# Latent attention's steps two at a time: shared rotary scores, three rotating bank pairs, four probability buffers

## The chip, the core and the metric

The kernel runs on one core of one Trainium2 chip. Time is the device time of one execution in microseconds. TensorE multiplies matrices into PSUM, which has eight banks of 512 float32 per partition; VectorE and ScalarE work element by element; GpSimd is hardly used here; SyncE issues the transfers. Each engine runs its own queue in order, and engines wait for each other by semaphores.

## What is computed

Four layers on x of 512 tokens by 1024 channels, in float32: a sparse-attention mixer and a latent-attention mixer, each followed by a gated feed-forward layer, then a gated delta rule and a gated linear attention, each with layer norm. The change lies in the attention of the second mixer: 8 heads, causal, with a key of 128 channels plus 64 rotary channels and a value of 128.

```python
def mla_mixer(h, k, v, w_q_a, q_a_norm, w_q_b, q_norm, w_out, cos, sin):
    ...
    q = jnp.concatenate([q[..., :QK_NOPE], apply_rope(q[..., QK_NOPE:], cos, sin)], axis=-1)
    scale = (QK_NOPE + QK_ROPE) ** -0.5
    ...
    def block(s0):
        t = s0 + jnp.arange(Q_BLOCK)
        qb = lax.dynamic_slice_in_dim(q, s0, Q_BLOCK, axis=1)
        s = jnp.einsum('bqhd,bkhd->bhqk', qb, k).astype(jnp.float32) * scale
        p = masked_softmax(s, kpos[None, :] <= t[:, None])
        o = jnp.einsum('bhqk,bkhd->bqhd', p.astype(v.dtype), v)
        return o.reshape(B, Q_BLOCK, MLA_HEADS * MLA_V)
    ...
    return o @ w_out
```

## The kernel before

The order of all work is written out by hand, one function per layer and engine: `pe_mla`, `act_mla`, `dve_mla`. A wait names a semaphore and a count. The attention runs in `M_STEPS` = 16 steps. A step v is a pair of heads (`ab` 0 and 1) and a tile t of 128 query tokens; it has n = (t + 1) x 128 keys. `m_step(v)` (L1981) gives for the four head pairs t = 0, 1, 2, 3, then 3, 2, 1, 0, then both again. So the steps have 128, 256, 384, 512, 512, 384, 256, 128 keys, twice over.

A step passes through nine pieces of work:

- TensorE `scores(v)` (L2106): per head one product over the 128 plain channels (L2119, "nope"), then one over the 64 rotary channels in pieces of up to 256 keys (L2124). The rotary rows of the two heads lie in partitions 0 to 63 and 64 to 127, and their matmuls start within 7 ns of each other. A float32 product is two instructions in the trace and one in the program's order. Signals `m_scores`.
- VectorE `biased(v)` (L2503): adds the mask, copies the scores from PSUM to the buffer `mprob[v % 3]` and takes the least value per row (L2509); then a small product (L2512) that signals `m_biased`.
- ScalarE `exps(v)` (L2295): two exponentials with their sums (L2300).
- VectorE `weighted(v)` (L2514): reciprocal of the sum (L2517) and scaling (L2519). Signals `m_weighted`.
- TensorE `turn(v)` (L2127): 2 (t + 1) transposes of 128 x 128 (L2137).
- ScalarE `turned(v)` (L2304): copies them from PSUM to `mpT[v % 2]` (L2309). Signals `m_pT`.
- TensorE `values(v)` (L2140): the product with the values (L2151), 4 (t + 1) instructions in the trace, into bank 6 or 7. It waits for `m_pT` and for `m_o_split` v - 1, which is `lower_o(v - 2)`. Signals `m_valued`.
- ScalarE `upper_o(v)` (L2311, instruction L2314) and VectorE `lower_o(v)` (L2522, instruction L221, `late_parts<-ps`): the result split in a high and a low part. `lower_o` signals `m_o_split`.

Beside these, `upper_out(v)` on ScalarE (L2316, instruction L2321) and `lower_out(v)` on VectorE (L2528, instruction L221, `panel_parts`) split a sixteenth of the weights of the output projection per step. `lower_out(v)` waits for `upper_out(v)`. The output projection (`out`, L2167) follows on TensorE right behind `values(15)`.

Scores lie in bank pair 0-1 or 2-3 in turn, transposes in 4-5. The order on TensorE is scores(v + 2), turn(v), values(v - 1); on ScalarE exps(v + 1), turned(v), upper_o(v - 1), upper_out(v); on VectorE weighted(v), biased(v + 2), lower_o(v - 2), lower_out(v - 1).

Of the kernel before, what the change touches and what calls it, by code (L numbers as in the profile page):

```python
# [104 lines left out]
def build_in(nc, io, ctx):  # L105
# [1815 lines left out]
    mmin, mbias, msum = [[take(2) for _ in range(3)] for _ in range(3)]  # L1921
# [3 lines left out]
    mprob = [hT[:, 2 * b:2 * b + 2, :] for b in range(3)]  # L1925
# [78 lines left out]
    def pe_mla(pe):  # L2004
# [101 lines left out]
        def scores(v):  # L2106
            pair, t, n = m_step(v)
            if v == 0:
                pe.wait_ge(S("m_dve_saved"), TT + 1)
                pe.wait_ge(S("m_q_out"), TT + 1)  # L2110
            elif v == 1:
                pe.wait_ge(S("m_dve_saved"), TT + 2)
                pe.wait_ge(S("m_q_out"), TT + 2)
            else:
                pe.wait_ge(S("m_biased"), v - 1)
            if v == 2 * TT:
                pe.wait_ge(S("m_dve_saved"), 2 * TT)
            for ab in range(2):
                mm(ps[:, 2 * (v % 2) + ab, 0:n], qTn[:, 2 * pair + ab, tokens(t)], kTn[:, 2 * pair + ab, 0:n], start=True, stop=False, skip_group_check=True)  # L2119
            for c in range(0, n, SPAN):  # L2120
                keys = slice(c, min(c + SPAN, n))
                for ab in range(2):
                    r = slice(ab * ROPE, (ab + 1) * ROPE)
                    last = mm(ps[:, 2 * (v % 2) + ab, keys], qTr[r, pair, tokens(t)], kTr[r, pair, keys], start=False, stop=True, skip_group_check=True)  # L2124
            last.then_inc(S("m_scores"), 1)

        def turn(v):  # L2127
            pair, t, n = m_step(v)
            pe.wait_ge(S("m_weighted"), v + 1)
            if v == 0:  # L2130
                pe.wait_ge(S("m_dve_saved"), TT + 3)
                pe.wait_ge(S("m_q_out"), TT + 3)
            else:
                pe.wait_ge(S("m_pT"), v)
            for ab in range(2):
                for kt in range(t + 1):
                    last = nc.tensor.transpose(ps[:, 4 + ab, tokens(kt)], mprob[v % 3][:, ab, tokens(kt)], ident[:])  # L2137
            last.then_inc(S("m_prob_turned"), 1)
# [52 lines left out]
    def act_mla(act):  # L2191
# [103 lines left out]
        def exps(v):  # L2295
            pair, t, n = m_step(v)
            act.wait_ge(S("m_biased"), v + 1)
            for ab in range(2):
                h = 2 * pair + ab
                last = nc.scalar.activation(mprob[v % 3][:, ab, 0:n], mprob[v % 3][:, ab, 0:n], ACT.Exp, bias=mbias[v % 3][:, ab:ab + 1],  # L2300
                                            scale=q_ninv[:, t, h:h + 1], accum_out=msum[v % 3][:, ab:ab + 1])
            last.then_inc(S("m_exp"), 1)

        def turned(v):  # L2304
# [4 lines left out]
            nc.scalar.copy(mpT[v % 2][:, :, 0:n], ps[:, 4:6, 0:n]).then_inc(S("m_pT"), 1)  # L2309
# [44 lines left out]
    def dve_mla(dve, link, lower):  # L2354
# [148 lines left out]
        def biased(v):  # L2503
            pair, t, n = m_step(v)
            wait_apart(dve, "m_scores", v + 1)
            if v >= 3:
                wait_apart(dve, "m_prob_turned", v - 2)
            for ab in range(2):
                last = nc.vector.tensor_tensor_reduce(out=mprob[v % 3][:, ab, 0:n], in0=ps[:, 2 * (v % 2) + ab, 0:n], in1=causal[:, T - n:T], scale=1.0, scalar=3e38,  # L2509
# [2010 lines left out]
```

## Time and profile before

| | us |
|---|---|
| median of 3 runs (2049.18 to 2051.91) | 2049.36 |
| the profiled execution, its own time | 2050.57 |
| its span, first to last instruction | 2048.8 |
| TensorE matmuls busy, of the span | 2016.0 (98%) |
| VectorE busy | 1412.9 (69%) |
| ScalarE busy | 969.6 (47%) |
| mean granted clock of TensorE | 0.996 |
| attention steps: first score matmul starts | 788.10 |
| attention steps: first output matmul starts | 848.25 |

Matmuls overlap in the pipeline: each shows its whole passage, so that an engine that is shown busy may still start its matmuls farther apart than they need. The distance from one start to the next tells what a matmul costs, and the idle time what a wait costs beyond that. A granted clock of 1.00 is 2.4 GHz, one of 0.50 is 1.2 GHz.

### The profile page before, as it was taken

How to read it: one execution, taken by the hardware profiler on the slowest of the kernel's cores; microseconds unless marked ns; L12 is line 12 of the kernel's file. 1: busy time of each engine (PE TensorE's matmuls, PEld its weight loads, DVE VectorE, ACT ScalarE, POOL GpSimd, SP SyncE). 2: the span in 40 equal slices, each digit the busy share in tenths (PEclk: the TensorE clock that was granted, in tenths of full speed). 3: DMA queues.
4: the chain of work that ended last, by engine and by line, in shares of the span. 5: the costliest groups of instructions: out<-in, count | busy, mean ns of one | idle time of the engine just before them, and what ended most of it. 6: DMA issues, size and time to landing. Idle time of an engine off the chain costs nothing. (4 is left out here: it accounts for less than half of the span.)

```text
span 2048.8 us, 36832 instructions
## 1 busy us (share of the span) xinstructions
PE 2016.0 (98%) x14803; PEld 1757.7 (86%) x14803; DVE 1412.9 (69%) x2747; ACT 969.6 (47%) x1874; POOL 148.3 (7%) x136
## 2 busy tenths in 40 slices
PE   9999999999999999999999999999999999999997
PEld 8997877999988877789999887888888888788986
DVE  5248865988865677578887556776667666586566
ACT  5337973555400266545553004554434454466554
POOL 1113320000000400000000002000000000020000
PEclk9999999999999999999999999999999999999999
DMA  5240001333232221022333321211112110212211
GB/s 189 83 145 22 2 2 65 111 104 103 94 124 96 97 70 60 22 82 93 104 107 113 109 94 67 88 63 62 61 61 72 53 59 20 91 53 102 81 44 42
DMA packets 30664, 159.35 MB, mean 78 GB/s; under 512 B 3392, under 2 KB 3904, under 8 KB 17856
## 3 DMA queue, kind: packets, MB, share of 16 engines
q1 hardware_dynamic: 30240, 157.24, 21.7%
q8 instruction: 97, 1.59, 0.3%
q14 instruction: 39, 0.32, 0.1%
q10 hardware_dynamic: 288, 0.20, 0.0%
HBM read 155.33 MB, written 2.10 MB: 77 GB/s over the span
## 5 line engine op out<-in xcount | busy, mean ns | idle before, releaser
L231 PE MATMUL ps<-late_parts,panel_upper 128*128 128x256 f32 (+1 forms) x1376 | 458.6, 333 | 0.0
L230 PE MATMUL ps<-late_parts,panel_upper 128*128 128x256 f32 (+1 forms) x1260 | 430.5, 342 | 3.8 <-issue 1.8
L232 PE MATMUL ps<-late_parts,panel_parts 128*128 128x256 f32 (+1 forms) x1260 | 424.3, 337 | 0.0
L221 DVE TENSOR_TENSOR panel_parts<-panel_sb,panel_upper 128x512 fp32r<-128x512 f32 (+1 forms) x330 | 321.1, 999 | 13.9 <-ACT panel_upper L768 8.4
L230 PE MATMUL ps<-panel_upper,hT_parts 128*128 128x256 f32 (+2 forms) x964 | 295.3, 306 | 2.2 <-DVE h_lower L961 1.4
L232 PE MATMUL ps<-panel_upper,h_lower 128*128 128x256 f32 (+2 forms) x964 | 283.7, 294 | 0.0
L231 PE MATMUL ps<-panel_parts,hT_parts 128*128 128x256 f32 (+2 forms) x964 | 282.3, 293 | 0.0
L231 PEld LDWEIGHTS ps<-late_parts,panel_upper 128*128 128x128 f32 x1376 | 258.7, 188 | 25.8
L230 PEld LDWEIGHTS ps<-late_parts,panel_upper 128*128 128x128 f32 x1260 | 236.7, 188 | 34.6 <-issue 4.5
L232 PEld LDWEIGHTS ps<-late_parts,panel_parts 128*128 128x128 f32 x1260 | 237.8, 189 | 28.6
L230 PE MATMUL ps<-hT_parts,panel_upper 128*128 128x512 f32 (+1 forms) x492 | 191.8, 390 | 1.7 <-PEq L4326 1.7
L230 PEld LDWEIGHTS ps<-panel_upper,hT_parts 128*128 128x128 f32 x964 | 183.0, 190 | 6.9 <-issue 3.2
L232 PE MATMUL ps<-hT_parts,panel_parts 128*128 128x512 f32 (+1 forms) x492 | 186.1, 378 | 0.0
L232 PEld LDWEIGHTS ps<-panel_upper,h_lower 128*128 128x128 f32 x964 | 183.2, 190 | 3.0
L231 PEld LDWEIGHTS ps<-panel_parts,hT_parts 128*128 128x128 f32 x964 | 182.2, 189 | 3.5
L231 PE MATMUL ps<-h_lower,panel_upper 128*128 128x512 f32 x416 | 165.8, 399 | 0.0
L1626 ACT CAST panel_upper<-panel_sb 128x512 fp32r<-128x512 f32 x230 | 132.3, 622 | 19.2 <-DVE panel_sb L1747 11.0
L230 PEld LDWEIGHTS ps<-hT_parts,panel_upper 128*128 128x128 f32 x492 | 92.3, 188 | 25.0 <-issue 3.9
L232 PEld LDWEIGHTS ps<-hT_parts,panel_parts 128*128 128x128 f32 x492 | 92.4, 188 | 19.5
L231 PEld LDWEIGHTS ps<-h_lower,panel_upper 128*128 128x128 f32 x416 | 78.2, 188 | 17.3 <-issue 0.2
L901 ACT ACTIVATE arena_sb<-arena_sb 128x384 f32<-128x384 f32 (+3 forms) x128 | 70.5, 553 | 9.0 <-DVE arena_sb L1160 8.7
L3206 DVE SCALAR_TENSOR_TENSOR arena_sb<-ps,arena_sb 128x511 f32<-128x511 f32 (+2 forms) x96 | 71.9, 748 | 3.4
(544 smaller groups left out, 3693.9 us busy)
## 6 DMA issues: line engine op xcount, KB each, us to landing
panel_sb<-ffn_gate_up_w SPq DMA_DIRECT2D x76, 512.0 KB, 4.5
panel_sb<-gdn_w SPq DMA_DIRECT2D x24, 1024.0 KB, 4.8
panel_sb<-ffn_down_w SPq DMA_DIRECT2D x22, 1024.0 KB, 4.8
panel_sb<-nsa_w SPq DMA_DIRECT2D x13, 1024.0 KB, 4.8
panel_sb<-gla_w SPq DMA_DIRECT2D x12, 1024.0 KB, 4.9
panel_sb<-gdn_out_w SPq DMA_DIRECT2D x8, 1024.0 KB, 4.9
panel_sb<-ffn_gate_up_w SPq DMA_DIRECT2D x6, 1024.0 KB, 4.9
panel_sb<-nsa_out_w SPq DMA_DIRECT2D x4, 1024.0 KB, 4.8
```

Source lines behind the costliest of these rows:

```text
L221: return engine.tensor_tensor(out, src, hi.bitcast(F32), ALU.subtract)
L230: mm(out, w_hi, x_hi, start=start, stop=False, skip_group_check=skip_group_check)
L231: mm(out, w_hi, x_lo, start=False, stop=False, skip_group_check=skip_group_check)
L232: return mm(out, w_lo, x_hi, start=False, stop=stop, skip_group_check=skip_group_check)
L901: nc.scalar.activation(prob[v % NB][:, ab, at:at + n], prob[v % NB][:, ab, at:at + n], ACT.Exp, bias=pmin[v % NB][:, k:k + 1], scale=-1.0, ...
L1626: nc.scalar.copy(hi, plain).then_inc(S("ffn_high"), 1)
L3206: last = nc.vector.scalar_tensor_tensor(conv[n][:, back:T], src[:, 0:T - back], hconv[:, n, 3 - back:4 - back], conv[n][:, back:T], ALU.mu ...
```

## The change

Two steps form a block. TensorE issues both nope products, then both steps' rotary products, then both groups of transposes, then two groups of values. Each use of a bank pair, scores or transposes, takes the next of three pairs (banks 0 to 5) in the order in which TensorE comes to them; `await_pair` waits for the release of the use three before: `m_biased` where that was scores, `m_pT` where it was transposes. There are four buffers `mprob` and four sets of the small sums. ScalarE and VectorE issue their pieces in twos as well. No instruction is added or removed.

The core of the diff (the changes that only put `MB` for 3 in an index are left out, except in `biased`):

```diff
+    MB = 4
+    mmin, mbias, msum = [[take(2) for _ in range(MB)] for _ in range(3)]
...
+    M_TURN, M_SCORE = "turn", "score"
+    M_SHARED = [(M_SCORE, 0), (M_SCORE, 1)]
+    for two in range(0, M_STEPS, 2):
+        M_SHARED += [(M_SCORE, v) for v in (two + 2, two + 3) if v < M_STEPS] + [(M_TURN, two), (M_TURN, two + 1)]
+    M_BANKS = {use: 2 * (n % 3) for n, use in enumerate(M_SHARED)}
+
+    def await_pair(pe, use):
+
+        n = M_SHARED.index(use)
+        if n < 3:
+            pe.wait_ge(S("m_dve_saved"), TT + 1 + n)
+            pe.wait_ge(S("m_q_out"), TT + 1 + n)
+            return
+        kind, v = M_SHARED[n - 3]
+        if kind == M_SCORE:
+            pe.wait_ge(S("m_biased"), v + 1)
+        else:
+            pe.wait_ge(S("m_pT"), v + 1)
...
+        def scores(*steps):
+            for v in steps:
+                pair, t, n = m_step(v)
+                await_pair(pe, (M_SCORE, v))
+                if v == 2 * TT:
+                    pe.wait_ge(S("m_dve_saved"), 2 * TT)
                 for ab in range(2):
...
+                    mm(ps[:, M_BANKS[M_SCORE, v] + ab, 0:n], qTn[:, 2 * pair + ab, tokens(t)], kTn[:, 2 * pair + ab, 0:n], start=True, stop=False, skip_group_check=True)
+            for v in steps:
+                pair, t, n = m_step(v)
+                for c in range(0, n, SPAN):
+                    keys = slice(c, min(c + SPAN, n))
+                    for ab in range(2):
+                        r = slice(ab * ROPE, (ab + 1) * ROPE)
+                        last = mm(ps[:, M_BANKS[M_SCORE, v] + ab, keys], qTr[r, pair, tokens(t)], kTr[r, pair, keys], start=False, stop=True, skip_group_check=True)
+                last.then_inc(S("m_scores"), 1)
...
-        for v in range(M_STEPS):
+        for v in range(0, M_STEPS, 2):
             if v + 2 < M_STEPS:
-                scores(v + 2)
+                scores(v + 2, v + 3)
             turn(v)
-            if v >= 1:
+            turn(v + 1)
+            if v:
                 values(v - 1)
+            values(v)
         values(M_STEPS - 1)
...
         exps(0)
-        for v in range(M_STEPS):
-            if v + 1 < M_STEPS:
-                exps(v + 1)
-            turned(v)
-            if v >= 1:
+        exps(1)
+        for v in range(0, M_STEPS, 2):
+            for u in (v, v + 1):
+                if u + 2 < M_STEPS:
+                    exps(u + 2)
+                turned(u)
+            if v:
                 upper_o(v - 1)
+            upper_o(v)
             upper_out(v)
+            upper_out(v + 1)
         upper_o(M_STEPS - 1)
...
-            if v >= 3:
-                wait_apart(dve, "m_prob_turned", v - 2)
+            if v >= MB:
+                wait_apart(dve, "m_prob_turned", v - MB + 1)
...
-        for v in range(M_STEPS):
+        for v in range(0, M_STEPS, 2):
             weighted(v)
+            weighted(v + 1)
+            if v >= 4:
+                lower_o(v - 3)
+            if v >= 2:
+                lower_o(v - 2)
             if v + 2 < M_STEPS:
                 biased(v + 2)
-            if v >= 2:
-                lower_o(v - 2)
+                biased(v + 3)
             if v:
+                lower_out(v - 2)
                 lower_out(v - 1)
+        lower_out(M_STEPS - 2)
         lower_out(M_STEPS - 1)
-        lower_o(M_STEPS - 2)
-        lower_o(M_STEPS - 1)
+        for v in range(M_STEPS - 3, M_STEPS):
+            lower_o(v)
```

Line numbers shift: nope L2119 is L2133 in the changed kernel, rotary L2124 is L2140, transposes L2137 are L2149, values L2151 are L2163, ScalarE's exponentials L2300 are L2314, its copies L2309, L2314 and L2321 are L2323, L2328 and L2335, VectorE's L2509, L2517 and L2519 are L2527, L2535 and L2537.

TensorE, steps 4 and 5, before: scores(4), turn(2), values(1), scores(5), turn(3), values(2).

```order
L2119 MATMUL ps<-late_sb 128x512 x2
L2124 MATMUL ps<-arena_sb 128x256 x4
L2137 MATMUL ps<-ident_sb,hT_sb 128x128 x6
L2151 MATMUL ps<-arena_sb 128x128 x4
L2119 MATMUL ps<-late_sb 128x384 x2
L2124 MATMUL ps<-arena_sb 128x256 x2
L2124 MATMUL ps<-arena_sb 128x128 x2
L2137 MATMUL ps<-ident_sb,hT_sb 128x128 x8
L2151 MATMUL ps<-arena_sb 128x128 x6
```

Now, the block for v = 2, with scores(5) drawn ahead of turn(2).

```order
L2133 MATMUL ps<-late_sb 128x512 x2
L2133 MATMUL ps<-late_sb 128x384 x2
L2140 MATMUL ps<-arena_sb 128x256 x6
L2140 MATMUL ps<-arena_sb 128x128 x2
L2149 MATMUL ps<-ident_sb,hT_sb 128x128 x14
L2163 MATMUL ps<-arena_sb 128x128 x10
```

The rotary products of steps 4 and 5 stand together behind both nope products, then come both groups of transposes and both groups of values.

ScalarE, before, around the same steps: exps(3), turned(2), upper_o(1), upper_out(2), exps(4), turned(3), upper_o(2), upper_out(3).

```order
L2300 ACTIVATE hT_sb,arena_sb<-hT_sb,arena_sb 128x512 x2
L2309 COPY arena_sb<-ps 128x2x384
L2314 CAST late_parts<-ps 128x2x128
L2321 CAST panel_upper<-panel_sb 128x512
L2300 ACTIVATE hT_sb,arena_sb<-hT_sb,arena_sb 128x512 x2
L2309 COPY arena_sb<-ps 128x1024
L2314 CAST late_parts<-ps 128x2x128
L2321 CAST panel_upper<-panel_sb 128x512
```

Now, the block for v = 2: exps(4), turned(2), exps(5), turned(3), upper_o(1) and (2), upper_out(2) and (3).

```order
L2314 ACTIVATE hT_sb,arena_sb<-hT_sb,arena_sb 128x512 x2
L2323 COPY arena_sb<-ps 128x2x384
L2314 ACTIVATE hT_sb,arena_sb<-hT_sb,arena_sb 128x384 x2
L2323 COPY arena_sb<-ps 128x1024
L2328 CAST late_parts<-ps 128x2x128 x2
L2335 CAST panel_upper<-panel_sb 128x512 x2
```

turned(2), the copy of 2x384, has exps(3) ahead of it before and exps(4) now, and the splitting of two steps comes behind both copies.

VectorE, the end of the stretch, before: lower_out(12), weighted(14), lower_o(12), lower_out(13), weighted(15), lower_o(13), lower_out(14) and (15), lower_o(14) and (15).

```order
L221 TENSOR_TENSOR panel_parts<-panel_sb,panel_upper 128x512
L2517 RECIPROCAL arena_sb<-arena_sb 128x2
L2519 TENSOR_SCALAR hT_sb<-hT_sb,arena_sb 128x256 x2
L221 TENSOR_TENSOR late_parts<-ps,late_parts 128x2x128
L221 TENSOR_TENSOR panel_parts<-panel_sb,panel_upper 128x512
L2517 RECIPROCAL arena_sb<-arena_sb 128x2
L2519 TENSOR_SCALAR hT_sb<-hT_sb,arena_sb 128x128 x2
L221 TENSOR_TENSOR late_parts<-ps,late_parts 128x2x128
L221 TENSOR_TENSOR panel_parts<-panel_sb,panel_upper 128x512 x2
L221 TENSOR_TENSOR late_parts<-ps,late_parts 128x2x128 x2
```

Now: lower_out(10) and (11), weighted(14), weighted(15), lower_o(11) and (12), lower_out(12) to (15), lower_o(13) to (15).

```order
L221 TENSOR_TENSOR panel_parts<-panel_sb,panel_upper 128x512 x2
L2535 RECIPROCAL arena_sb<-arena_sb 128x2
L2537 TENSOR_SCALAR hT_sb<-hT_sb,arena_sb 128x256 x2
L2535 RECIPROCAL arena_sb<-arena_sb 128x2
L2537 TENSOR_SCALAR hT_sb<-hT_sb,arena_sb 128x128 x2
L221 TENSOR_TENSOR late_parts<-ps,late_parts 128x2x128 x2
L221 TENSOR_TENSOR panel_parts<-panel_sb,panel_upper 128x512 x4
L221 TENSOR_TENSOR late_parts<-ps,late_parts 128x2x128 x3
```

lower_o(13) has moved behind lower_out(14) and lower_out(15).

## Rows read from the trace of the kernel before

**Rows 1.** Busy time: stretch, us, busy us (count) per engine, PEclk, DMA share, GB/s
```profile
806.00:842.00 36.00, 36.00 (x257) 27.93 (x256) 27.36 (x101) 28.12 (x68) 0.00 (x0) 1.00 0.01 1
1813.50:1816.90 3.40, 3.40 (x18) 3.40 (x17) 3.37 (x4) 2.85 (x4) 3.24 (x3) 0.50 0.00 0
```

**Rows 2.** Waits, 786 to 850 us: who waits for whom, total us, times, longest
```profile
DVE hT_sb L2509 <- PE ps L2124: 10.8, 13, 1.6
```

**Rows 3.** TensorE in time: start, us, line, count; L2119 nope, L2124 rotary, L2137 transposes, L2151 values
```profile
838.64 1.95 PE L2151 MATMUL ps<-arena_sb 128*128 128x128 f32 x16
840.43 0.61 PE L2119 MATMUL ps<-late_sb 128*128 128x128 f32 x4
840.97 0.49 PE L2124 MATMUL ps<-arena_sb 64*128 64x128 f32 x4
841.39 0.87 PE L2137 MATMUL ps<-ident_sb,hT_sb 128*128 128x128 f32 x6
842.10 1.95 PE L2151 MATMUL ps<-arena_sb 128*128 128x128 f32 x16
844.19 0.66 PE L2137 MATMUL ps<-ident_sb,hT_sb 128*128 128x128 f32 x4
844.68 1.50 PE L2151 MATMUL ps<-arena_sb 128*128 128x128 f32 x12
846.71 0.44 PE L2137 MATMUL ps<-ident_sb,hT_sb 128*128 128x128 f32 x2 [0.53 <-DVE hT_sb L2519]
846.99 1.50 PE L2151 MATMUL ps<-arena_sb 128*128 128x128 f32 x12
```

**Rows 4.** TensorE in time, three other places
```profile
793.90 0.44 PE L2137 MATMUL ps<-ident_sb,hT_sb 128*128 128x128 f32 x2 [0.24 <-DVE hT_sb L2519]
...
818.53 0.70 PE L2124 MATMUL ps<-arena_sb 64*128 64x256 f32 x4
...
825.10 1.14 PE L2124 MATMUL ps<-arena_sb 64*128 64x256 f32 x8
```

**Rows 5.** Groups by shape, 788 to 848.5 us: busy us, mean ns of one, idle before
```profile
L2300 ACT ACTIVATE hT_sb<-hT_sb,arena_sb 128x512 f32<-128x512 f32 x8 | 6.5, 812 | 0.0
...
L2300 ACT ACTIVATE hT_sb<-hT_sb,arena_sb 128x384 f32<-128x384 f32 x8 | 5.6, 702 | 0.0
L2509 DVE CUSTOM_DVE_ANT_0 hT_sb<-ps,arena_sb 128x512 f32<-128x512 f32 x8 | 5.2, 689 | 3.7 <-PE ps L2124 3.7
L2300 ACT ACTIVATE hT_sb<-hT_sb,arena_sb 128x256 f32<-128x256 f32 x8 | 4.7, 592 | 0.0
...
L2509 DVE CUSTOM_DVE_ANT_0 hT_sb<-ps,arena_sb 128x384 f32<-128x384 f32 x8 | 4.1, 555 | 1.6 <-PE ps L2124 1.6
...
L2309 ACT COPY arena_sb<-ps 128x768 f32<-128x768 f32 x4 | 3.2, 791 | 2.1 <-PE ps L2137 2.1
L2509 DVE CUSTOM_DVE_ANT_0 hT_sb<-ps,arena_sb 128x256 f32<-128x256 f32 x8 | 3.2, 423 | 2.7 <-PE ps L2124 2.6
...
L2509 DVE CUSTOM_DVE_ANT_0 hT_sb<-ps,arena_sb 128x128 f32<-128x128 f32 x8 | 2.0, 289 | 2.9 <-PE ps L2124 2.9
...
L2309 ACT COPY arena_sb<-ps 128x256 f32<-128x256 f32 x4 | 1.5, 372 | 1.3 <-PE ps L2137 1.3
```

**Rows 6.** VectorE in time: one biased of 512 keys, and the stretch's end
```profile
826.54 0.69 DVE L2509 CUSTOM_DVE_ANT_0 hT_sb<-ps,arena_sb 128x512 f32<-128x512 f32 x1 [0.70 <-PE ps L2124]
...
827.89 0.16 DVE L2512 TENSOR_TENSOR arena_sb<-arena_sb 128x2 f32<-128x2 f32 x1
...
849.01 0.69 DVE L221 TENSOR_TENSOR panel_parts<-panel_sb,panel_upper 128x512 fp32r<-128x512 f32 x1 [1.08 <-ACT panel_upper L2321]
849.62 0.75 DVE L221 TENSOR_TENSOR late_parts<-ps,late_parts 128x256 fp32r<-128x256 f32 x2
```

**Rows 7.** ScalarE in time: upper_o and upper_out at the stretch's end
```profile
848.08 0.37 ACT L2314 CAST late_parts<-ps 128x256 fp32r<-128x256 f32 x1 [0.52 <-PE ps L2151]
848.35 0.63 ACT L2321 CAST panel_upper<-panel_sb 128x512 fp32r<-128x512 f32 x1
```

More of the change, by code:

```diff
@@ L1924, in build_in @@
     rope_b = h_raw[:, 6, :]
-    mprob = [hT[:, 2 * b:2 * b + 2, :] for b in range(3)]
+    mprob = [hT[:, 2 * b:2 * b + 2, :] for b in range(MB)]
     mpT = [h_raw[:, 2 * b:2 * b + 2, :] for b in range(2)]
@@ L2129, in turn @@
             pe.wait_ge(S("m_weighted"), v + 1)
[L2130 to L2134, printed above, removed]
+            await_pair(pe, (M_TURN, v))
             for ab in range(2):
                 for kt in range(t + 1):
-                    last = nc.tensor.transpose(ps[:, 4 + ab, tokens(kt)], mprob[v % 3][:, ab, tokens(kt)], ident[:])
+                    last = nc.tensor.transpose(ps[:, M_BANKS[M_TURN, v] + ab, tokens(kt)], mprob[v % MB][:, ab, tokens(kt)], ident[:])
             last.then_inc(S("m_prob_turned"), 1)
@@ L2308, in turned @@
                 act.wait_ge(S("m_valued"), v - 1)
-            nc.scalar.copy(mpT[v % 2][:, :, 0:n], ps[:, 4:6, 0:n]).then_inc(S("m_pT"), 1)
+            nc.scalar.copy(mpT[v % 2][:, :, 0:n], ps[:, M_BANKS[M_TURN, v]:M_BANKS[M_TURN, v] + 2, 0:n]).then_inc(S("m_pT"), 1)
         def upper_o(v):
@@ L2505, in biased @@
             wait_apart(dve, "m_scores", v + 1)
-            if v >= 3:
-                wait_apart(dve, "m_prob_turned", v - 2)
+            if v >= MB:
+                wait_apart(dve, "m_prob_turned", v - MB + 1)
             for ab in range(2):
-                last = nc.vector.tensor_tensor_reduce(out=mprob[v % 3][:, ab, 0:n], in0=ps[:, 2 * (v % 2) + ab, 0:n], in1=causal[:, T - n:T], scale=1.0, scalar=3e38,
-                                                      op0=ALU.add, op1=ALU.min, accum_out=mmin[v % 3][:, ab:ab + 1])
+                last = nc.vector.tensor_tensor_reduce(out=mprob[v % MB][:, ab, 0:n], in0=ps[:, M_BANKS[M_SCORE, v] + ab, 0:n], in1=causal[:, T - n:T], scale=1.0, scalar=3e38,
+                                                      op0=ALU.add, op1=ALU.min, accum_out=mmin[v % MB][:, ab:ab + 1])
             link(last)
-            nc.vector.tensor_tensor(mbias[v % 3], mmin[v % 3], q_inv[:, t, 2 * pair:2 * pair + 2], ALU.mult).then_inc(S("m_biased"), 1)
+            nc.vector.tensor_tensor(mbias[v % MB], mmin[v % MB], q_inv[:, t, 2 * pair:2 * pair + 2], ALU.mult).then_inc(S("m_biased"), 1)
         def weighted(v):
@@ L2516, in weighted @@
             dve.wait_ge(S("m_exp"), v + 1)
-            link(nc.vector.reciprocal(msum[v % 3], msum[v % 3]))
+            link(nc.vector.reciprocal(msum[v % MB], msum[v % MB]))
             for ab in range(2):
-                last = nc.vector.tensor_scalar(mprob[v % 3][:, ab, 0:n], mprob[v % 3][:, ab, 0:n], msum[v % 3][:, ab:ab + 1], None, ALU.mult)
+                last = nc.vector.tensor_scalar(mprob[v % MB][:, ab, 0:n], mprob[v % MB][:, ab, 0:n], msum[v % MB][:, ab:ab + 1], None, ALU.mult)
             last.then_inc(S("m_weighted"), 1)
```

24 lines of the change are left out of this document (2 added, 22 removed).

## The prediction, made before the changed kernel had run

> **What bounds the kernel now.** I read the stretch in which the changed lines run, from the first score matmul (788.1 us) to the first output matmul (848.2 us), in four views: busy time by stretch, the waits, TensorE's instructions in time, and the groups of each tile shape. In the middle 36 us TensorE is busy for all 36 at the full clock, VectorE for 27 and ScalarE for 28 [rows 1]. VectorE is the one that waits, 13 times, for the last rotary matmul of a step [rows 2]. So TensorE bounds the stretch: what is taken off its queue shortens the kernel, and what makes it wait lengthens it. After the stretch its matmuls follow on without a gap, so I carry a shift here to the end whole.
>
> Busy is not the same as streaming. Four score matmuls of 128 columns take 840.43 to 840.97, 0.54 us, where 16 value matmuls of 128 columns take 838.64 to 840.43, 0.112 each, so four should take 0.45 [rows 3]. The 0.09 is the step from 128-row matmuls to 64-row ones. The rotary group of four 256-column matmuls takes 0.70 and that of eight 1.14 [rows 4]: two more pairs cost 0.44, 0.22 a pair. So a pair streams at 0.11 per 128 columns. But two pairs of 128 hold the engine from 840.97 to 841.39, 0.42 instead of 0.22 [rows 3]: 0.20 more, which goes, as the group of eight shows no more of it than that of four, to the start of the group and the way back. The first transpose costs 0.05 more than the next: two take 0.28 (846.71 to 846.99), and six against four 0.71 against 0.49, so 0.11 each [rows 3]. One excursion into rotary matmuls and back costs 0.09 + 0.20 + 0.05, with roundings 0.35 us.
>
> **What the change removes.** Before there are 16 excursions, one per step. Steps 0 and 1 keep theirs, the other 14 share seven: 7 x 0.35 = **-2.46 us**. If half of the 0.20 is paid again at the second step, it is -1.8. The trace shows it once in a group of two pairs and once in one of four [rows 3, 4], so I take the whole.
>
> The Trainium skill, "TensorEngine Tiling (Array Packing)", Key Properties, says that a change of tiling mode drains TensorE. By that rule alone a switch would cost the last matmul's depth, which I estimate from the matmul groups as 0.275 - 0.112 = 0.16, two per excursion, and the removal would be 2.3 instead of 2.46; the trace agrees in kind, and its number is used.
>
> TensorE's own idle time before is small: 0.24 and a late load, together 0.30, ahead of the first transposes (793.90) [rows 4], 2.09 - 1.79 = 0.30 ahead of those of step 14, and 2.03 - 12 x 0.112 = 0.69 ahead of those of step 15 [rows 3]. In the new order more matmuls lie ahead of all three. **-1.29 us**.
>
> **What it adds: a chain inside each block.** The block for steps v, v+1 is on TensorE: scores(v+2, v+3), turn(v), turn(v+1), values(v-1), values(v). Two of its parts now need something that starts only when rotary scores of this very block are done. turn(v+1) takes the bank pair of scores(v+2), so it waits for biased(v+2). values(v) waits for the copy turned(v), which on ScalarE stands behind exps(v+2), which needs biased(v+2). Before, values(v) had the scores and transposes of a later step between it and its copy, which is why TensorE did not wait.
>
> The chain's links, d being the group's mean [rows 5]. A semaphore from the last rotary matmul to VectorE: 0.30 (group ends 826.24, biased starts 826.54) [rows 4, 6]. biased to its signal: 2d + 0.13 (826.54 to 828.05 = 1.51 with d = 0.689) [rows 6]; so 0.71, 0.98, 1.24, 1.51 us for 128 to 512 keys. exps: 2d, 1.18, 1.40, 1.62 from 256 keys on. The copy 0.37 (step of 128 keys) or 0.79 (384). Hand-overs 0.03 and 0.06. The last matmul ends 0.17 after its slot. Against it stands cover: the other step's rotary (0.11 per 128 keys and pair), 0.15 for the way back (half of the 0.20, and the 0.05), transposes at 0.11, values at 0.112.
> - Block 0 (step 2: 384 keys): 0.17+0.30+1.24+0.03+1.40+0.37+0.06 = 3.57 against 0.86+0.15+6x0.11 = 1.67: 1.90 of waiting.
> - Block 2 (step 4: 512 keys): 0.17+0.30+1.51+0.03+1.62+0.79+0.06 = 4.48 against 0.64+0.15+14x0.11+8x0.112 = 3.23: 1.25.
> - Block 4 (step 6: 256 keys): turn(5) waits for biased(6), 0.17+0.30+0.98+0.06 = 1.51 against 0.21+0.15+8x0.11 = 1.24: 0.27; values(4) then comes out even.
> - Block 6 (step 8: 128 keys): turn(7), 1.24 against 0.43+0.15+4x0.11 = 1.02: 0.22, values(6) about as much: 0.25.
> - Block 8 is block 0 with 4 value matmuls more: 1.45. Blocks 10 and 12 repeat 2 and 4: 1.25, 0.27.
> Together **+6.64 us**. VectorE has weighted(v), weighted(v+1) and two lower_o ahead of biased(v+2), ScalarE two upper_o and two upper_out ahead of exps(v+2); they run under the nope matmuls of scores(v+2), which is before this chain starts, so I cost them at nothing. If that cover went, it would be up to 1 us per block.
>
> **At the end**: values(15) needs lower_o(13) (`m_o_split` 14). Before, that stood among the steps. Now it is the first of three behind lower_out(14) and (15), and these wait for upper_out(14) and (15), which on ScalarE stand behind upper_o(14), which waits for values(14). So values(15) waits for a round trip that starts at values(14). Links: copy 848.08 to the start of upper_out 848.35, 0.27 [rows 7]; a second upper_out 0.52 later, 0.63 to its end; VectorE 0.03 later; lower_out 0.61 to the start of lower_o (849.01 to 849.62) [rows 6]; lower_o 0.42; hand-overs 0.10; end of the last matmul 0.16: 2.74 less roundings, **+2.73 us**. Nothing on TensorE may pass it: the output matmuls are queued behind.
>
> **Small**: a matmul that waited has its weights loaded late, 0.05 for transposes; for values no such wait is in the trace, from 0 to 0.1. With 7 to 13 waits, and 0.15 at values(14) because ScalarE's queue is late: **+0.5**. The order of biased, the fourth buffer and the moved upper_out and lower_out of other blocks have slack on both engines: nothing, else at most 1 us in all.
>
> Sum: -2.46 - 1.29 + 6.64 + 2.73 + 0.5 = **+6.1 us**. On the profiled execution, 2050.57, that is 2056.7; it lies 1.2 above the median of the runs, so 2055.5. A measurement of this kernel can tell about 0.2% (4.1 us) from no change.
>
> **Rivals.** (A) The waits are covered: ScalarE and VectorE have 8 us of 36 free, and biased may get the scores early enough. Then only the removals stay, -3.75: 2045.6, within 0.2%. It needs each chain shorter than its cover; the rows say longer in all seven blocks. 0.05. (B) Not slower by what can be told: in blocks 0, 2, 8 and 10, which hold 5.85 of the 6.64, the chain overlaps with the cover more than I sum, biased(v+2) running under the second step's rotary and exps(v+2) under the first transposes. With 1 us less in each, -3.75 + 2.64 + 2.73 + 0.5 = +2.1: 2051.5; it decides from 0.5 us less in each. Against it: every link is a semaphore wait on the one before. 0.14. (C) The change doesn't do what it says: the second step of a shared group pays its entry again, so nothing is removed: 2055.5 + 2.5 = 2058. The group of eight argues against it. 0.07. (D) TensorE's clock. It is granted in full here [rows 1]; pauses could bring it to 1.2 GHz, as it is in the 3.4 us from 1813.5 [rows 1], behind a stretch that is outside this change. Matmuls then stream at half the rate, so one such dip costs half of itself, 1.7, and two 3.4: 2057.2 to 2058.9. 0.12. The Trainium skill, "TensorE: Matmul & The Clock Gate", PE-mode transpose, says that transposes don't count as busy for the clock. By that rule the longer runs of transposes with pauses around them would make (D) likelier; against it the trace grants the full clock through this stretch with its transposes in it [rows 1].
>
> **Numbers.** Forecast 0.62, with its own range 2053.5 to 2057.6 (0.3 us either way per block); A 0.05, B 0.14, C 0.07, D 0.12. The range over the cases but A and part of B: 2051.8 to 2059.2. Slower by over 0.2% needs 2053.46: C, D and nearly all of the forecast, 0.80. Same: A, B and the rest, 0.18. Faster, 0.02, needs more than the whole removal.
>
> **What the new profile would show.** The score line in seven runs of shared rotary matmuls, one 0.20 each; TensorE idle ahead of values(0), (2), (8), (10) by 0.6 to 1.3 us with ScalarE's copy as releaser, ahead of turn(1), (3), (9), (11) by about 0.6 with VectorE's biased; and one pause of about 2.7 ahead of the last four value matmuls, released by VectorE. The first output matmul at about 854.4 instead of 848.2. If values(v) starts without a wait, my chain is wrong; if the pause before values(15) is missing, my reading of `m_o_split` is.

## The result

| | before | changed |
|---|---|---|
| median of 5 runs, us | 2049.45 | 2059.95 |
| lowest to highest, us | 2049.18 to 2051.91 | 2057.78 to 2062.26 |
| profiled execution, us | 2050.57 | 2057.78 |
| its span, us | 2048.8 | 2056.0 |
| first score matmul to first output matmul | 788.10 to 848.25, 60.15 | 787.36 to 853.96, 66.60 |
| mean granted clock | 0.996 | 0.994 |

The change makes the kernel slower by 0.49%, ratio 1.0049 with a 95% interval of 1.0038 to 1.0061. The stretch that it rearranges is 6.45 us longer; the forecast said 6.1. The whole kernel is 10.5 us slower; the forecast said 6.1, and at most 9.8. Four microseconds of the medians are not in the stretch. The two profiled executions differ by 7.2 us alone: 6.45 in the stretch and 1.5 behind it, less 0.7 ahead of it, where the order of work is the same in both.

TensorE's instructions of the changed kernel in order of time, the view of [rows 3], for the blocks of v = 0 and v = 2 (start, us, line, shapes, count, idle before and who ended it; L2133 nope, L2140 rotary, L2149 transposes, L2163 values).

```profile
790.61 3.17 PE L2133 MATMUL ps<-late_sb 128*128 128x384 f32 x8
793.72 1.79 PE L2140 MATMUL ps<-arena_sb 64*128 64x256 f32 x16
795.43 0.44 PE L2149 MATMUL ps<-ident_sb,hT_sb 128*128 128x128 f32 x2
796.22 0.63 PE L2149 MATMUL ps<-ident_sb,hT_sb 128*128 128x128 f32 x4 [0.35 <-DVE arena_sb L2530]
797.91 0.71 PE L2163 MATMUL ps<-arena_sb 128*128 128x128 f32 x4 [1.06 <-ACT arena_sb L2323]
798.46 3.17 PE L2133 MATMUL ps<-late_sb 128*128 128x512 f32 x8
801.56 1.79 PE L2140 MATMUL ps<-arena_sb 64*128 64x256 f32 x16
803.28 0.87 PE L2149 MATMUL ps<-ident_sb,hT_sb 128*128 128x128 f32 x6
804.66 1.06 PE L2149 MATMUL ps<-ident_sb,hT_sb 128*128 128x128 f32 x8 [0.50 <-DVE arena_sb L2530]
805.56 1.06 PE L2163 MATMUL ps<-arena_sb 128*128 128x128 f32 x8
806.99 1.60 PE L2163 MATMUL ps<-arena_sb 128*128 128x128 f32 x12 [0.37 <-ACT arena_sb L2323]
```

The same view of the kernel before, for step 4 (512 keys):

```profile
797.99 1.88 PE L2119 MATMUL ps<-late_sb 128*128 128x512 f32 x4
799.80 1.13 PE L2124 MATMUL ps<-arena_sb 64*128 64x256 f32 x8
800.87 0.87 PE L2137 MATMUL ps<-ident_sb,hT_sb 128*128 128x128 f32 x6
```

The two blocks shown have one rotary group of 16 each, as they should. In the block for v = 0, steps 2 and 3 together have 3.10 us of nope and 1.72 us of rotary matmuls, 4.82 up to the first transpose. Before, a step of 512 keys took 2.88 (800.87 less 797.99) and one of 384 keys 2.26, so 5.14 for two. Behind them stand the new waits: 0.35 ahead of turn(1) (released by L2530, the end of biased(2)) and 1.06 ahead of values(0) (released by the copy L2323), then 0.50 ahead of turn(3) and 0.37 ahead of values(2). The idle times start at the modelled end of the last matmul. By starts the waits are longer: 797.91 less 796.22 is 1.69 us, of which four transposes need 0.47, so values(0) waited 1.22.

The waits of the stretch, in the view of [rows 2]:

```profile
ACT hT_sb L2314 <- DVE arena_sb L2530: 16.8, 7, 3.7
...
PE ps L2163 <- DVE late_parts L221: 2.7, 1, 2.7
...
PE ps L2163 <- ACT arena_sb L2323: 2.4, 4, 1.1
PE ps L2149 <- DVE arena_sb L2530: 2.2, 6, 0.5
```

TensorE waits 7.3 us in three kinds, and ScalarE, which had waited for TensorE's transposes before, now waits 16.8 us for biased: exps(v+2) stands at the head of its queue. Before, the others waited for TensorE [rows 2]; now all three wait for each other in turn.

The end of the stretch, TensorE:

```profile
848.13 2.65 PE L2163 MATMUL ps<-arena_sb 128*128 128x128 f32 x20
853.52 0.68 PE L2163 MATMUL ps<-arena_sb 128*128 128x128 f32 x4 [2.73 <-DVE late_parts L221]
853.96 0.48 PE L230 MATMUL ps<-late_parts,panel_upper 128*128 128x512 f32 x1
854.27 0.39 PE L231 MATMUL ps<-late_parts,panel_upper 128*128 128x512 f32 x1
854.50 0.56 PE L232 MATMUL ps<-late_parts,panel_parts 128*128 128x512 f32 x1
854.86 0.63 PE L230 MATMUL ps<-late_parts,panel_upper 128*128 128x512 f32 x1
855.29 0.63 PE L231 MATMUL ps<-late_parts,panel_upper 128*128 128x512 f32 x1
```

20 value matmuls end, and the last four start 2.73 us after. Then ScalarE and VectorE over the same time, against [rows 6, 7]:

```profile
850.82 0.37 ACT L2328 CAST late_parts<-ps 128x256 fp32r<-128x256 f32 x1 [0.45 <-PE ps L2163]
851.09 1.14 ACT L2335 CAST panel_upper<-panel_sb 128x512 fp32r<-128x512 f32 x2
```

```profile
851.75 1.29 DVE L221 TENSOR_TENSOR panel_parts<-panel_sb,panel_upper 128x512 fp32r<-128x512 f32 x2 [1.85 <-ACT panel_upper L2335]
852.96 0.75 DVE L221 TENSOR_TENSOR late_parts<-ps,late_parts 128x256 fp32r<-128x256 f32 x2
```

ScalarE starts upper_o(14) at 850.82 and two upper_out at 851.09; VectorE starts lower_out(14) and (15) at 851.75 and lower_o(13) at 852.96; values(15) goes at 853.52. That is the round trip of the forecast, link by link.

And there is what the forecast did not count. The output matmuls start 0.23 us apart at 854.27 (L231) and 0.43 apart from 854.86 on. The busy time of two stretches shows why (columns as in [rows 1], the clock third from the end):

```profile
806.00:842.00 36.00, 33.35 (x235) 26.25 (x233) 26.25 (x90) 26.44 (x68) 0.00 (x0) 1.00 0.01 1
...
854.60:858.00 3.40, 3.40 (x10) 2.66 (x9) 0.42 (x1) 0.01 (x1) 0.00 (x0) 0.50 0.00 0
```

In the 36 us in the middle the clock is full, as in [rows 1], with 2.65 us of idle TensorE in them. From 854.6 on it is granted at 0.50, 1.2 GHz, for 3.4 us; such a fall is called a dip here. One microsecond earlier TensorE had ended a wait of 2.7 us. From the first output matmul to the last instruction the kernel before took 1200.5 us and this execution 1202.0.

### The profile page after: what moved, and what is told of

Same layout as the page of the kernel before. It is cut to its first block and busy times, and to the rows that moved or that the text cites. A ratio compares the mean times of both kernels' runs of the same rounds, so it can differ in the third digit from the quotient of the medians.

```text
span 2056.0 us, 36832 instructions
## 1 busy us (share of the span) xinstructions
PE 2018.3 (98%) x14803; PEld 1761.5 (86%) x14803; DVE 1412.9 (69%) x2747; ACT 968.0 (47%) x1874; POOL 148.3 (7%) x136
## 5 line engine op out<-in xcount | busy, mean ns | idle before, releaser
L231 PE MATMUL ps<-late_parts,panel_upper 128*128 128x256 f32 (+1 forms) x1376 | 459.3, 334 | 0.0
L231 PE MATMUL ps<-panel_parts,hT_parts 128*128 128x256 f32 (+2 forms) x964 | 282.3, 293 | 0.0
L231 PEld LDWEIGHTS ps<-late_parts,panel_upper 128*128 128x128 f32 x1376 | 259.1, 188 | 26.0
L231 PEld LDWEIGHTS ps<-panel_parts,hT_parts 128*128 128x128 f32 x964 | 182.2, 189 | 3.4
L231 PE MATMUL ps<-h_lower,panel_upper 128*128 128x512 f32 x416 | 165.8, 398 | 0.0
L231 PEld LDWEIGHTS ps<-h_lower,panel_upper 128*128 128x128 f32 x416 | 78.2, 188 | 17.3 <-issue 0.2
```

The lines of the kernel that those rows point to most:

```text
L231: mm(out, w_hi, x_lo, start=False, stop=False, skip_group_check=skip_group_check)
```

## The experiments

The length of the stretch was read as above, from the first score matmul to the first output matmul. In the table the column "before" is the median of the kernel before on the same chip: e1 to e4 were measured on one chip, r_after and e5 to e7 on another. "Beyond the stretch" is what the kernel is slower by, less what its stretch is longer by. The 95% intervals of the ratios reach 1.8 to 2.8 us to either side, so a single value of that column says little, and only the kernels taken together do. The last column is the mean of the granted clock over a kernel's executions; for the kernel before it was 0.9953 beside e1 to e4 and 0.9952 beside the others. "Stretch" comes from the one profiled execution; in e3_before_tail and e6_copy_first 0.4 us of it is a dip that began before the first output matmul.

| kernel | stretch, us | against before | time, us | before | slower by | beyond the stretch | mean clock |
|---|---|---|---|---|---|---|---|
| changed, first set | 66.60 | +6.45 | 2059.95 | 2049.45 | 10.5 | +4.0 | 0.9932 |
| changed, again (r_after) | 66.62 | +6.47 | 2058.36 | 2050.27 | 8.1 | +1.6 | 0.9944 |
| e3_before_tail | 63.52 | +3.37 | 2055.28 | 2049.80 | 5.5 | +2.1 | 0.9935 |
| e6_copy_first | 65.90 | +5.75 | 2058.33 | 2050.27 | 8.1 | +2.3 | 0.9938 |
| e4_unshared | 63.44 | +3.29 | 2054.49 | 2049.80 | 4.7 | +1.4 | 0.9942 |
| e1_tail | 64.06 | +3.91 | 2054.11 | 2049.80 | 4.3 | +0.4 | 0.9947 |
| e2_filled | 66.60 | +6.45 | 2056.35 | 2049.80 | 6.5 | +0.1 | 0.9950 |
| e5_unshared_tail | 60.90 | +0.75 | 2050.68 | 2050.27 | 0.4 | -0.3 | 0.9956 |
| e7_lagged | 58.66 | -1.49 | 2048.84 | 2050.27 | -1.4 | +0.1 | 0.9954 |

### e1_tail: lower_o(13) back ahead of the last two lower_out

```diff
+        lower_o(M_STEPS - 3)
         lower_out(M_STEPS - 2)
         lower_out(M_STEPS - 1)
-        for v in range(M_STEPS - 3, M_STEPS):
+        for v in range(M_STEPS - 2, M_STEPS):
             lower_o(v)
```

> The changed kernel with lower_o(13) moved ahead of lower_out(14) and lower_out(15) on VectorE, and nothing else. Theory: the pause of 2.7 us ahead of values(15) goes (0.2 stays), and with it the stretch of 3.4 us at the granted clock 0.50 right behind it, which cost about 1.5. The stretch from the first score matmul to the first output matmul takes 64.0 us instead of 66.6; the time is 4.1 below the changed kernel's, about 2056. Rival, the clock falls because of all the pauses and the grouped transposes together: the stretch at 0.50 stays, and the time falls by 2.6 alone, to about 2057.4. Second rival, the executions above 2058 lose their time elsewhere: their spread of 2057.8 to 2062.3 stays as wide.

Measured: 2054.11 us (2053.19 to 2056.32), ratio to before 1.0024 with an interval of 1.0015 to 1.0033, stretch 64.06. TensorE at the end:

```profile
847.75 2.65 PE L2163 MATMUL ps<-arena_sb 128*128 128x128 f32 x20
850.59 0.68 PE L2163 MATMUL ps<-arena_sb 128*128 128x128 f32 x4 [0.19 <-DVE late_parts L221]
851.03 0.48 PE L230 MATMUL ps<-late_parts,panel_upper 128*128 128x512 f32 x1
```

One line on VectorE takes the pause from 2.73 to 0.19 us and the stretch from 66.60 to 64.06, as expected to 0.1 us. The granted clock behind it is 1.00. The kernel is slower than before by 4.3 us, which is 6.2 less than the first set of the changed kernel and 3.8 less than the second; 4.1 was expected. The spread is 3.1 us against 4.5 in the first set, but the second set of the changed kernel has 3.1 too, so that nothing follows from it.

### e2_filled: the pause filled with matmuls that wait for nothing

```diff
             values(v)
+        keep_going(4, 12)
         values(M_STEPS - 1)
```

`keep_going(bank, n)` is the kernel's own helper: n matmuls of 128 columns into a bank that nobody reads.

> The changed kernel with 12 matmuls of 128 columns without use put between values(14) and values(15) on TensorE, which fill 2.6 of the 2.7 us of the pause and wait for nothing. Theory: the pause is as long as before in the program's sense, so the stretch stays at 66.6 us, but the clock stays at 1.00 behind it: 1.5 us less than the changed kernel, and less spread between executions. Rival, the pause has nothing to do with the clock: a stretch at 0.50 is still there behind values(15), and the time is the changed kernel's within 0.5 us.

Measured: 2056.35 us (2055.18 to 2058.17), ratio 1.0033 (1.0021 to 1.0045), stretch 66.60, to the hundredth that of the changed kernel. Busy time in and behind the former pause:

```profile
851.00:854.10 3.10, 3.05 (x29) 2.89 (x27) 1.96 (x4) 1.37 (x3) 0.00 (x0) 1.00 0.00 0
854.10:857.50 3.40, 3.40 (x18) 2.77 (x17) 0.42 (x1) 0.37 (x1) 0.00 (x0) 1.00 0.00 0
```

values(15) starts as late as before, yet the clock behind it stays at 1.00: 18 matmuls in 3.4 us where the changed kernel had 10. The kernel is slower than before by about what the stretch is longer (6.5, with an interval of 4.3 to 9.2, against 6.45). By the medians the work without use in the pause is worth 4.0 us against the first set of the changed kernel and 1.6 against the second; the second of these is within the noise. The useless matmuls changed no wait. One trace with a full clock would not be enough, as r_after below shows; it is the traces and medians of all kernels together that carry the reading.

### e3_before_tail: the kernel before with the end of the changed one

```diff
-            if v >= 2:
+            if 2 <= v < M_STEPS - 1:
                 lower_o(v - 2)
...
         lower_out(M_STEPS - 1)
+        lower_o(M_STEPS - 3)
         lower_o(M_STEPS - 2)
...
-            upper_out(v)
+            if v < M_STEPS - 2:
+                upper_out(v)
+        upper_out(M_STEPS - 2)
+        upper_out(M_STEPS - 1)
```

> The kernel before, with the end of the attention alone ordered as in the changed kernel: lower_o(13) behind lower_out(14) and (15) on VectorE, upper_out(14) and (15) behind upper_o(14) on ScalarE. Theory: values(15) waits 2.7 to 2.8 us; the stretch grows from 60.15 to 63.0, and the clock falls to 0.50 behind it for 3.4 us, 1.5 more: 2053.8 against 2049.5 for the kernel before. Rival, the dip needs the pauses in the blocks as well: 2052.4, with the clock full behind the stretch.

Measured: 2055.28 us (2054.78 to 2056.35), ratio 1.0030 (1.0020 to 1.0041), stretch 63.52. Its last value matmuls and the first output matmul, and the busy time from the pause on:

```profile
850.00 1.19 PE L2151 MATMUL ps<-arena_sb 128*128 128x128 f32 x4 [2.73 <-DVE late_parts L221]
850.84 0.77 PE L230 MATMUL ps<-late_parts,panel_upper 128*128 128x512 f32 x1
```

```profile
848.70:852.10 3.40, 2.10 (x7) 1.94 (x8) 1.91 (x5) 0.38 (x2) 0.00 (x0) 0.50 0.00 0
852.10:855.50 3.40, 3.40 (x9) 2.63 (x9) 0.00 (x0) 0.00 (x0) 0.00 (x0) 0.50 0.00 0
```

The pause is the same 2.7, and here the clock is granted at 0.50 for 6.8 us, of which 1.3 lie inside the pause; 3.4 were expected, and the time came out at 2055.3 instead of 2053.8. Steps 14 and 15 of this kernel have waits of their own before it [rows 3]. So a few instructions in another place cost an otherwise untouched kernel 5.5 us. Of the 3.4 in the stretch 0.4 is the clock too: from the last value matmuls to the first output matmul are 0.84 us, where the changed kernel has 0.44. That leaves 3.0 for the wait and 2.5 for what lies beyond it. The dip needs none of the pauses in the blocks.

### e4_unshared: each step's rotary matmuls behind its nope matmuls

```diff
-            for v in steps:
-                pair, t, n = m_step(v)
-                for c in range(0, n, SPAN):
+                for c in range(0, n, SPAN):
```

> The changed kernel with the rotary matmuls of a step right behind its own nope matmuls again, blocks, banks, buffers and all else as changed. Theory: the 2.46 us of the seven saved excursions come back, but biased(v+2) gets its scores 0.5 to 1.8 us earlier, so that the chains of 6.6 us in the blocks shrink to about 1.1; the pause of 2.7 ahead of values(15) stays, with the dip of the clock behind it. The stretch takes 62.8 us instead of 66.6, 3.8 less than the changed kernel. So sharing the rotary matmuls costs more than it saves. Rival, the waits come from the order of ScalarE and VectorE and from the three rotating pairs, not from where the rotary matmuls stand: the waits stay at 6.6 and the stretch takes 69 us.

Measured: 2054.49 us (2053.22 to 2057.69), ratio 1.0025 (1.0016 to 1.0034), stretch 63.44. The block for v = 0 (L2138 rotary, L2147 transposes, L2161 values):

```profile
789.73 1.46 PE L2133 MATMUL ps<-late_sb 128*128 128x384 f32 x4
791.12 0.92 PE L2138 MATMUL ps<-arena_sb 64*128 64x256 f32 x8
791.97 1.98 PE L2133 MATMUL ps<-late_sb 128*128 128x512 f32 x4
793.88 1.13 PE L2138 MATMUL ps<-arena_sb 64*128 64x256 f32 x8
794.95 0.87 PE L2147 MATMUL ps<-ident_sb,hT_sb 128*128 128x128 f32 x6
795.93 0.71 PE L2161 MATMUL ps<-arena_sb 128*128 128x128 f32 x4
```

The wait ahead of turn(1) is gone: six transposes run through in 0.87 us. From the first transpose to values(0) are 0.98 us, where the changed kernel took 2.48. biased(2) now gets its scores before the nope matmuls of step 3. The stretch is 3.2 us shorter than the changed kernel's, though it pays the seven excursions again; 3.8 were expected. The difference is a cost that the expectation had not counted: a nope group right behind a rotary group takes 0.10 us more (791.97 to 793.88, 1.91, against 1.81 behind transposes or values in the kernel before), seven times. By starts, sharing saves 3.0 us against this order and costs 6.1 in waits. That is the core of the case. The clock was at 0.50 behind this kernel's pause too:

```profile
850.40:853.80 3.40, 3.40 (x9) 2.66 (x9) 0.42 (x1) 0.17 (x1) 0.00 (x0) 0.50 0.00 0
```

### r_after: the changed kernel again

> The changed kernel once more, on the same chip as the runs beside it. Its stretch from first score to first output matmul was 66.6 us against 60.15, 6.45 more, but its five executions were 10.5 above the kernel before. Theory: the rest is TensorE's clock, which falls behind the pause ahead of values(15), once (3.4 us at 0.50, 1.5 us lost) or twice and in some executions behind the pauses of the blocks as well: median 2058.5 to 2060.5 with a mean granted clock of 0.993, 0.002 to 0.003 below the kernel before. Rival, the five executions were a chip's or an hour's accident: the median is 2050 + 6.45 + 1.5 = 2057.8 or less, and the mean clock 0.995.

Measured: 2058.36 us (2056.38 to 2059.45), ratio 1.0038 (1.0025 to 1.0052), stretch 66.62. The profiled execution took 2056.38, the shortest of all of this kernel, and behind its pause, the same 2.7 us, stands:

```profile
854.20:857.60 3.40, 3.40 (x18) 2.77 (x17) 0.42 (x1) 0.37 (x1) 0.00 (x0) 1.00 0.02 5
```

18 matmuls, the clock at 1.00. The dip behind the pause comes in some executions and not in others. What it costs is read where VectorE adds the first output of the projection; the two rows are of the changed kernel's first profile and of this one:

```profile
865.58 0.69 DVE L1459 TENSOR_TENSOR xT_sb<-xT_sb,ps 128x512 f32<-128x512 f32 x1 [10.51 <-PE ps L232]
```

```profile
864.30 0.69 DVE L1459 TENSOR_TENSOR xT_sb<-xT_sb,ps 128x512 f32<-128x512 f32 x1 [8.97 <-PE ps L232]
```

From the first output matmul (853.96 and 854.22) to there are 11.62 us with the dip and 10.08 without: 1.54 us. The traces of the kernel before, e1, e2, e5 and e7, which have no dip there, show 10.08 as well, e4 11.63, e3 12.20 and e6 11.05, these two with 0.4 more inside the stretch. So the dip is there in four of the five traces with an unfilled pause of 2.7 us, and in none of the five without one. To the end of the kernel the two executions differ by 1.6 us, but that is no second reading of the same dip: this one has a dip at 1275 that the other lacks, and the other has three of them around 1800 where this one has one.

The expectation was met in part: the median, 2058.4, lies between the theory's 2058.5 and the rival's 2057.8, and the mean clock, 0.9944, between the two values named. Both sets are slower than the 6.45 us of the stretch explain, by 4.0 and 1.6 us.

### e5_unshared_tail: both causes taken away

The edits of e1_tail and e4_unshared together.

> The changed kernel with the rotary matmuls of each step right behind its nope matmuls and with lower_o(13) ahead of lower_out(14) and (15): the two suspected causes taken away, the blocks, banks and buffers left. Theory: the two effects add, 66.60 - 3.2 - 2.5 = 60.9 us for the stretch, within 1 us of the kernel before, the clock full behind it, and the time within 0.1% of the kernel before, 2050.5. Rival, something else of the change costs (the three rotating pairs, ScalarE's and VectorE's new order): the stretch stays above 62.5 and the time above 2052.5.

Measured: 2050.68 us (2049.76 to 2051.76), ratio 1.0001 (0.9992 to 1.0010), stretch 60.90, where 60.9 was expected. All idle time of TensorE in the stretch is 0.61 us.

The two effects add. Nothing else of the change (three rotating bank pairs, four buffers, blocks of two on three engines) costs anything that the time shows. The stretch is still 0.75 us longer than before; the seven nope groups right behind rotary groups, 0.10 each as in e4, are of that size.

### e6_copy_first: turned(u) ahead of exps(u + 2)

```diff
             for u in (v, v + 1):
+                turned(u)
                 if u + 2 < M_STEPS:
                     exps(u + 2)
-                turned(u)
```

> The changed kernel with turned(u) ahead of exps(u + 2) on ScalarE, nothing else. Theory: values(v) no longer waits for biased(v + 2) and exps(v + 2), so the waits ahead of values(0), (2), (8), (10), 3.4 us in all, go; those ahead of turn(1), (3), (9), (11), 0.5 each, stay, since they hang on the bank pair; later exponentials cost up to 1.5 again ahead of turn(5), (13), (15). The stretch takes 64.8 us instead of 66.6. The pause ahead of values(15) and the dip of the clock behind it stay. Rival, ScalarE's queue is not what values(v) waits for: the waits stay at 3.4 and the stretch at 66.6.

Measured: 2058.33 us (2055.97 to 2060.22), ratio 1.0038 (1.0025 to 1.0052), stretch 65.90, only 0.7 us shorter instead of 1.8. TensorE in blocks 0 and 2:

```profile
796.60 0.63 PE L2149 MATMUL ps<-ident_sb,hT_sb 128*128 128x128 f32 x4 [0.35 <-DVE arena_sb L2530]
797.06 0.61 PE L2163 MATMUL ps<-arena_sb 128*128 128x128 f32 x4
798.01 3.27 PE L2133 MATMUL ps<-late_sb 128*128 128x512 f32 x8 [0.34 <-DVE arena_sb L2530]
...
804.32 0.95 PE L2149 MATMUL ps<-ident_sb,hT_sb 128*128 128x128 f32 x7 [0.51 <-DVE arena_sb L2530]
```

values(0) now follows the transposes at once (797.06), which shows that it was ScalarE's queue it had waited for. But the nope matmuls of step 4 then wait 0.34 for biased(3), and turn(1) and turn(3) wait as before. The wait moved on to the next thing that hangs on biased, and late exponentials cost turn(5) and turn(13) 0.64 us of idle time each instead of 0.18, and turn(15) 0.40. I had priced the move of the wait with too little. Of 3.4 us taken away 2.7 seem to have come back, but 0.4 of that is the clock: a dip began at 852.4, inside the pause, so that from the last value matmuls to the first output matmul are 0.84 us instead of 0.44. At the full clock the stretch would be 1.1 us shorter than the changed kernel's.

### e7_lagged: shared groups, with the values a whole block later

```diff
-    mpT = [h_raw[:, 2 * b:2 * b + 2, :] for b in range(2)]
+    mpT = [h_raw[:, 2 * b:2 * b + 2, :] for b in range(MB)]
...
             if v + 2 < M_STEPS:
                 scores(v + 2, v + 3)
+            if v:
+                values(v - 2)
             turn(v)
-            turn(v + 1)
             if v:
                 values(v - 1)
-            values(v)
+            turn(v + 1)
+        values(M_STEPS - 2)
         values(M_STEPS - 1)
...
         for v in range(0, M_STEPS, 2):
-            for u in (v, v + 1):
-                if u + 2 < M_STEPS:
-                    exps(u + 2)
-                turned(u)
+            if v:
+                upper_o(v - 2)
+            turned(v)
+            if v + 2 < M_STEPS:
+                exps(v + 2)
             if v:
                 upper_o(v - 1)
-            upper_o(v)
+            if v + 2 < M_STEPS:
+                exps(v + 3)
+            turned(v + 1)
             upper_out(v)
             upper_out(v + 1)
+        upper_o(M_STEPS - 2)
         upper_o(M_STEPS - 1)
...
-            if v >= 4:
-                lower_o(v - 3)
-            if v >= 2:
-                lower_o(v - 2)
...
                 lower_out(v - 2)
+                lower_o(v - 2)
                 lower_out(v - 1)
+                lower_o(v - 1)
         lower_out(M_STEPS - 2)
         lower_out(M_STEPS - 1)
-        for v in range(M_STEPS - 3, M_STEPS):
+        for v in range(M_STEPS - 2, M_STEPS):
             lower_o(v)
```

> A version that keeps the shared rotary matmuls and moves the rest around them: four buffers mpT instead of two, values a whole block later (scores(v+2, v+3), values(v-2), turn(v), values(v-1), turn(v+1) on TensorE; upper_o(v-2), turned(v), exps(v+2), upper_o(v-1), exps(v+3), turned(v+1), two upper_out on ScalarE; two weighted, two biased, then lower_out and lower_o in turn on VectorE). Theory: the chains get two groups of values as cover, the saving of 2.46 us for the seven shared excursions and the 1.3 us of idle time before come through: the stretch takes 57.2 us against 60.15 in the kernel before, and the time is 3 us below it, 2047. Rival, the chains of a shared group cannot be covered, since scores(v + 4) waits for biased(v + 3) when no values are left between: the stretch stays at 60 us or more and the time at 2050.

Measured: 2048.84 us (2046.17 to 2050.57), ratio 0.9992 (0.9983 to 1.0001), stretch 58.66. A block in the middle of the stretch:

```profile
826.52 3.27 PE L2133 MATMUL ps<-late_sb 128*128 128x512 f32 x8 [0.17 <-DVE arena_sb L2536]
829.73 1.79 PE L2140 MATMUL ps<-arena_sb 64*128 64x256 f32 x16
831.44 0.71 PE L2163 MATMUL ps<-arena_sb 128*128 128x128 f32 x4
831.99 0.82 PE L2149 MATMUL ps<-ident_sb,hT_sb 128*128 128x128 f32 x6
832.65 1.06 PE L2163 MATMUL ps<-arena_sb 128*128 128x128 f32 x8
```

The values of the block before lie between the rotary group and turn(v + 1), and cover the chain: from 829.73 on nothing waits. The shared groups stay. The stretch is 1.5 us shorter than in the kernel before and 7.9 shorter than in the changed one; 3 and 9.4 were expected. What is left is the rival of that expectation in small: scores(4) and scores(12) wait for biased of the step before, 0.79 and 0.17 us (the second is the one in the fence), and turn(1) waits 0.35, 1.3 us of idle time in all. The time is 1.4 us below before, and the interval just includes no difference.

## Why the prediction was wrong

**What bounds the kernel**: right. Everything that TensorE waited in the stretch came through to the end, and e5 shows that work moved on the other two engines costs nothing that the time shows.

**The excursions, -2.46**: right in sign and in size. Steps 2 and 3 alone gained 0.32 up to the first transpose, and the 0.05 of one first transpose: over seven blocks about 2.6 by starts. The stretch of e5, with one excursion per step, is 60.90 with 0.61 idle, that of e7, with shared ones, 58.66 with 1.30: 2.9 between them without the idle time, of which 0.7 is e5's own (its nope groups behind rotary groups). Rival C, that nothing is saved, fell.

**Idle time that goes, -1.29**: right, none of the three waits of [rows 3, 4] is left.

**The chains, +6.64**: right, block by block. By starts, block 0 waits 0.51 + 1.22 us and loads weights late by 0.13, 1.86 against 1.90; block 2 1.33 against 1.25; block 4 0.38 against 0.27. Over all seven it is 7.1 instead of 6.6, the late loads among it. Rival A (covered) and rival B (half covered) fell; e4 shows that the cause is the one named, and e6 that the copy behind exps is the second half of it.

**The end, +2.73**: right, 2.9 us by starts; e1 took it away with one line.

**Sum of the stretch, +6.1**: 6.45 measured. The new profile showed each thing that the forecast had named for it, but the idle times ahead of values(2), (8) and (10), 0.37 to 0.62, were mostly shorter than the 0.6 to 1.3 named; by starts the sum fits.

**The step that failed is rival D, TensorE's clock.** The prediction gave it a chance of 0.12, priced it as one or two dips of 1.7 us on top of a sum that had none, and put its end at 2058.9 and the range's at 2059.2. In fact the dip behind the pause belongs to the likeliest case: it is in four of the five traces that have this pause, at 1.5 us each where the rival had 1.7. Over the kernels with the pause unfilled the time beyond the stretch is 1.4 to 4.0 us, over those without it or with it filled -0.3 to 0.4, and the mean clock goes with it, 0.993 to 0.994 against 0.995 to 0.996. The forecast had a pause of 2.73 us in its own sum and put nothing behind it. It looked at the clock in the stretch before [rows 1], where TensorE had no pause over 0.7 us, and held the full clock there against rival D. That row could not say so. It says that the transposes do no harm, and this held: in the changed kernel the clock is full through the blocks of transposes and waits of 0.3 to 1.2 us, and falls behind the one of 2.7. The rule of the Trainium skill that made rival D likelier, that transposes don't count as busy ("TensorE: Matmul & The Clock Gate", PE-mode transpose), was not what decided: e2 fills the same pause with plain matmuls and leaves all transposes where they are, and the clock holds in the profile and on the mean.

Had the term been +2.7 (the middle of 1.4 and 4.0), the forecast had been 2058.2 and the range, moved with it, had held the result. But the dip seen in the traces is worth 1.5 us, and with 1.5 alone the forecast had been 2057.0, 3.0 us below the result. The rest of the first set's 4.0 is clock as well, by an estimate from clocks that are listed to 0.001: its mean of 0.9932 against 0.9953 (the value of the kernel before beside e1 to e4; beside the first set none is on record) is 8.6 us more at half clock in an execution, and at 1.54 us for 3.4 that is 3.9; for the second set, 0.9944 against 0.9952, it is 1.5 against the 1.6 measured. Where in the first set's executions that clock was lost is open, since only one of them has a trace. Dips in other layers come and go from execution to execution: the kernel before has two of 3.4 us between 1789 and 1817 in its trace, the changed kernel has three there in its first profile and one in its second, with one more at 1275.

So part of the miss is luck of the set. The second set's median, 2058.4, lies inside the range, 8.1 us above the kernel before of its own chip; against it the missing term would not have shown in the time.

## What to carry to other kernels

Putting like matmuls together saves TensorE's switches, here about 0.36 us each, but every result of the group comes later, and whoever needs the first of them waits for the whole group: count the chain from the first result against the cover that is left before grouping. Look at the last step of a rearranged loop by itself; one small operation behind two that it does not need cost 2.7 us there. And a pause of TensorE can have a second price behind it: where one of such a length can't be avoided, try matmuls without use in it. Here 12 of them (24 instructions) in 2.7 us left the stretch as long as it was, and the clock behind them stayed full. No other length of pause was tried.

## What the runs showed of the hardware

- A pause of 2.7 us of TensorE is followed by 3.4 us at a granted clock of 0.50 in the changed kernel and in e4_unshared. In e6_copy_first 3.4 us at 0.50 begin inside the pause, in e3_before_tail 6.8 us do. In r_after, which has the same pause, there are none: whether the dip comes is not fixed by the program. Pauses of 0.3 to 1.2 us with work between them were followed by none in any trace of this case in this stretch.
- At 0.50 the matmuls of 512 columns started 0.43 us apart instead of 0.23, and one such dip of 3.4 us cost 1.54 us (11.62 against 10.08 us from the first output matmul to VectorE's first addition behind it).
- In a shared rotary group the change from one step's matmuls to the next one's costs nothing: 16 instructions take 1.72 us for 7 times 128 keys, each of them two pairs of matmuls at 0.11 us, 1.54 in all, with about 0.20 once. The pairs belong to different steps and banks.
- A nope group that stands right behind a rotary group takes 0.10 us more than one behind values or transposes (1.91 against 1.81 us for 512 keys, e4_unshared and the kernel before).
- The first value matmul after a wait is 0.10 us slower than the next, the first transpose 0.03.
